# A decoder layer on one core: P times V of four pairs moved ahead of the last product of k, the last norms of three tiles in another form, the first job in another order

## The chip, the cores and the metric

The kernel runs on one core of one Trainium2 chip. The metric is the device time in microseconds (us) of one execution. Engines are named PE (TensorE), DVE (VectorE), ACT (ScalarE), POOL (GpSimd) and SP (SyncE, which here only starts transfers).

## The reference, cut to what matters

```python
h = layer_norm(concat([meta, x]), ln_emb_g, ln_emb_b)      # 16 + 512 tokens of width 1024
qa, ka, va, ga, qi, ki, wi, cq, ckv, kpe, gb = split(h @ w_in)
# branch b: latent attention, 8 heads, dense causal
qb = rms_norm(cq) @ w_uq ; kvb = rms_norm(ckv) @ w_ukv
ob = softmax(qb . kb * scale_b, causal) @ vb
# branch a: 8 heads over the 128 keys that an indexer (qi, ki, wi) picks for each query
la = qa . ka[sel] * scale_a + rel_bias ; oa = softmax(la) @ va[sel]
mixed = concat([oa * silu(ga), ob * silu(gb)])
out = layer_norm(ALPHA * h + mixed @ w_out, ln_post_g, ln_post_b)[:, 16:]
# layer_norm: (y - mean) * rsqrt(var + eps) * g + b, over 1024 columns
```

## The kernel before, in words

All of it is float32. A product of weights and hidden states is made of three products of rounded parts (high times high, high times low, low times high); the parts of the weights lie in `wh` and `wl`, those of the states in `hh` and `hl`. Weight blocks of 128 columns come by SP's queue, ACT makes the high part (line 596), POOL or DVE the low part (line 589). Every engine runs its own instructions in order, and all of them follow one list, `ORDER`, that `schedule()` writes by hand. The entries that matter here:

- `("J", kind, n, m)` is a job: products of PE (line 1503) into a PSUM bank, which ACT and DVE empty. A job of k, `("J", "ka", p, half)`, has 24 products of 264 columns. ACT empties it with four copies (line 935) and DVE with four subtractions (line 1202) into `ks`.
- `("S", g)` are the scores of head g. Heads 0 to 7 are the dense ones (line 1691), heads 8 to 15 the sparse ones (line 1695). DVE adds the mask and takes the minimum (line 1301), `("X", g)` is ACT's exponential, `("R", g)` POOL's division. The scores of an even sparse head wait, on PE, for all of ACT's and DVE's instructions of the last k job of its pair:

```python
                    if g >= HEADS and e == 0:
                        n = max(NJ["ka", p, 1], NJ["qa", p, 0]) + 1
                        pe.wait_ge(job_act, BY_ACT[n])
                        pe.wait_ge(job_dve, BY_DVE[n])
```

- `("TP", g)` and the job `tq` transpose P of head g on PE (lines 1710, 1715, 1717, 1557), and ACT and DVE copy it to `pt`. `("PV", pair, part)` is P times V of two heads, 20 products on PE (line 1740) into `ps_o`, which DVE multiplies with the gate (line 1331).

In the steps g = 7, 9, 11 and 13 the list runs: the products of k for the next pair (and of q, for g = 7), TP and tq of head g - 1, PV of pair 2, 3, 4 or 5, then the scores of the even head g + 1.

The first job (`cq`) is written out ahead of the list. Its states come in eight units of two chunks of 128 columns and two tiles of x. For a unit u PE transposes normed x (`spread`, line 1428), ACT or DVE applies the gain (lines 823, 1075), ACT rounds it (line 833), DVE makes the low part (line 1083). `high(u)` is four products with the high weights (line 1443) and four with the low weights (line 1448), `low(u)` four with the low states (line 1458). Units 4 to 7 need ACT's norm of x tiles 2 and 3 (line 815), and their transposes reuse the banks of units 0 to 3, so `spread(u)` waits for DVE's low part of unit u - 4.

At the end each tile t of 128 tokens takes four jobs `out` (4 to 7), added to `res` by DVE (line 1215), with statistics beside them (lines 1351, 1354, 1357, 1361, 1382). Tiles 0 and 1 then take: DVE reciprocal and minus mean times it (`nmr`, line 1376), ACT scale and shift (line 1034), POOL times gain (line 780), POOL plus bias (line 782). Tile 2 takes: DVE minus mean, times gain, in two halves (line 1369), DVE reciprocal (line 1372), ACT scale (line 1030), POOL plus bias (line 774). Tile 3 stays on DVE (lines 1389, 1392, 1397). SP sends the tiles out.

Of the kernel before, what the change touches and what calls it, by code (L numbers as in the profile page):

```python
# [21 lines left out]
ALU = mybir.AluOpType  # L22
# [9 lines left out]
QT = NQ // P  # L32
# [83 lines left out]
def schedule():  # L116
# [84 lines left out]
    for g in range(2 * HEADS):  # L201
        p = (g % HEADS) // 2
        more = p + 1 < PAIRS

        if g < HEADS:
            jobs = [("va", *va.pop(0)) for _ in range((1, 1, 2, 0, 2, 1, 2, 0)[g])]
            if g % 2 and more:
                jobs = [("qn", p + 1)] + jobs + [("kn", p + 1, 0), ("kn", p + 1, 1)]
                if g == 5:
                    jobs[1:3] = jobs[2:0:-1]  # L210
            if g == HEADS - 1:
                jobs = [("qa", 0), ("ka", 0, 0), ("ka", 0, 1)]
        elif more:
            jobs = [("ka", p + 1, 0), ("ka", p + 1, 1)] if g % 2 else [("qa", p + 1)]
        else:
            jobs = [("out", *outs.pop(0)) for _ in range(6 if g % 2 == 0 else 4)]
        pair = (g - 3) // 2 if g >= 3 and g % 2 else None
        late = pair is not None and g >= HEADS - 1 and more or g == HEADS - 1
        order.append(("S", g))
        if HEADS + 2 <= g < HEADS + 6:  # L220
            order.append(("MIXL", 4 + g - HEADS - 2))
        if g > HEADS and g % 2 and more:
            job(*jobs.pop(0), extra=0)
        if jobs[0][0] == "qn":
            order.append(("QPE", jobs[0][1]))
            job(*jobs.pop(0), extra=0)
        if pair is not None and not late and g < HEADS:
            order += [("PV", pair, 0), ("PV", pair, 1)]
        if g % 2 and g < HEADS - 1:
            while jobs:  # L230
                job(*jobs.pop(0), extra=0)
            pick(2)
        order.append(("X", g))
        if g < HEADS and (g % 2 == 0 or g == HEADS - 1):
            pick(1)
        if pair is not None and not late and g >= HEADS:
            order += [("PV", pair, 0), ("PV", pair, 1)]
        if g >= HEADS and not more:
            for _ in range(3 if g % 2 == 0 else 2):
                job(*jobs.pop(0), extra=int(g % 2 == 0))  # L240
        order.append(("R", g))
        if g == 2 * HEADS - 1:
            need(BLOCKS[0], 1)
        if HEADS <= g < 2 * HEADS - 2:
            order.append(("FOLD", g - HEADS + 2))
        if g < HEADS and g % 2 == 0:
            pick(2)
        if g == HEADS - 1:
            assert not halves
            order += [("MASK",), ("BIAS",), ("FOLD", 0), ("FOLD", 1)]  # L250
        for n, j in enumerate(jobs):
            job(*j, extra=int(j[0] == "out"))
        if g:
            order += [("TP", g - 1), ("J", "tq", g - 1, 0)]
        if late:
            order += [("PV", pair, 0), ("PV", pair, 1)]
        need(BLOCKS[0], 2)
        if HEADS + 1 <= g < HEADS + 5:
            order.append(("MIX", 4 + g - HEADS - 1))
        if g == 2 * HEADS - 2:  # L260
            order += [("MIX", 0), ("MIX", 1)]
# [72 lines left out]
def build(nc, x, meta, ln_emb_g, ln_emb_b, rel_bias, ln_post_g, ln_post_b, weights, gains, onehot, cos_t,  # L334
# [6 lines left out]
    with ctx:  # L341
# [3 lines left out]
        def sem(name):  # L345
            return ctx.enter_context(nc.semaphore(name))
# [118 lines left out]
        h_high = sem("h_high")  # L465
        h_high_act = sem("h_high_act")
        shift = sem("shift")
        ln_pool = sem("ln_pool")
        y_pool = sem("y_pool")
        h_low = sem("h_low")  # L470
        meta_s = sem("meta_s")
# [197 lines left out]
        def _(pool):  # L669
# [39 lines left out]
            for stage, *arg in ORDER:  # L709
# [48 lines left out]
                elif stage == "FOLD":  # L758
                    h = arg[0]
                    pool.wait_ge(bias_in[h], 16)  # L760
                    if h == 0:
                        pool.wait_ge(masked, QT + 1)
                    if h >= 2:
                        pool.wait_ge(s_min, 4 * (HEADS + h - 1))
                    for i in range(QT):
                        s = slice(POFF[i], POFF[i] + NK[i])
                        pool.tensor_tensor(bm[:, h % 2, s], bias[:, h % 4, T - NK[i]:T], mask[:, s],  # L767
                                           ALU.add).then_inc(folded, 1)
                elif stage == "LNC" and arg[0] == QT - 2:
                    t = arg[0]  # L770
                    y = res[:, t, :]
                    pool.wait_ge(post_in, 32)
                    pool.wait_ge(xn_done, t + 1)
                    pool.tensor_tensor(y, y, post_b, ALU.add).then_inc(y_pool, 1)
                elif stage == "LNC" and arg[0] < QT - 1:
                    t = arg[0]
                    y = res[:, t, :]
                    pool.wait_ge(post_in, 32)
                    pool.wait_ge(xn_done, t + 1)
                    pool.tensor_tensor(y, y, post_g, ALU.mult).then_inc(ln_pool, 1)  # L780
                    pool.wait_ge(ln_pool, t + 1)
                    pool.tensor_tensor(y, y, post_b, ALU.add).then_inc(y_pool, 1)


# [1 line left out]
        def _(act):  # L786
# [75 lines left out]
            for stage, *arg in ORDER:  # L862
# [154 lines left out]
                elif stage == "LNB":  # L1017
# [4 lines left out]
                    if t == QT - 1:  # L1022
                        a, b = LAST_PIECES[1]
                        act.wait_ge(y_done, 2)
                        act.dma_start(out[0, NQ - P:NQ, a:b], res[:, t, a:b]).then_inc(y_out, 16)
                    if t == QT - 2:
                        act.wait_ge(centred, 2)
                        act.wait_ge(shift, 7 + 2 * t + 1)
                        y = res[:, t, :]
                        act.activation(y, y, ACT.Identity, scale=rstd[:, t:t + 1]).then_inc(xn_done, 1)  # L1030
                    elif t < QT - 2:
                        act.wait_ge(shift, 7 + 2 * t + 2)
                        y = res[:, t, :]
                        act.activation(y, y, ACT.Identity, bias=nmr[:, t:t + 1], scale=rstd[:, t:t + 1]).then_inc(xn_done, 1)


        @block.vector
        def _(dve):
# [64 lines left out]
            stat(4, 1)  # L1103
            low(0)
            gains_of(3)
            inverse(4, 7)
            low(1)
            low(2)
            low(3)

# [20 lines left out]
            for stage, *arg in ORDER:  # L1131
# [226 lines left out]
                elif stage == "LNB" and arg[0] < QT - 1:  # L1358
# [2 lines left out]
                    dve.bn_stats(st[:, t, 1, :], res[:, t, 512:1024]).then_inc(bn_s, 1)  # L1361
                    dve.wait_ge(bn_s, 10 + 2 * t + 2)
                    dve.bn_aggr(mv[:, t, :], st[:, t, :, :].rearrange("p a b -> p (a b)")).then_inc(stats, 1)
                    if t == QT - 2:
                        dve.wait_ge(post_in, 32)
                        dve.wait_ge(stats, 5 + t + 1)
                        for n in range(2):
                            y = res[:, t, 512 * n:512 * n + 512]
                            dve.scalar_tensor_tensor(out=y, in0=y, scalar=mv[:, t, 0:1], in1=post_g[:, 512 * n:512 * n + 512],
                                                     op0=ALU.subtract, op1=ALU.mult).then_inc(centred, 1)  # L1370
                    dve.wait_ge(root, 8 + t + 1)
                    dve.reciprocal(rstd[:, t:t + 1], rstd[:, t:t + 1]).then_inc(shift, 1)
                    if t == QT - 2:
                        continue
                    dve.wait_ge(shift, 7 + 2 * t + 1)
                    dve.scalar_tensor_tensor(out=nmr[:, t:t + 1], in0=mv[:, t, 0:1], scalar=-1.0,
                                             in1=rstd[:, t:t + 1], op0=ALU.mult, op1=ALU.mult).then_inc(shift, 1)
                elif stage == "LNB":

                    t = QT - 1  # L1380
# [9 lines left out]
                                                 op0=ALU.subtract, op1=ALU.mult).then_inc(ln_s, 1)  # L1390
                    dve.wait_ge(root, 8 + t + 1)
                    dve.reciprocal(rstd[:, t:t + 1], rstd[:, t:t + 1]).then_inc(shift, 1)
                    dve.wait_ge(shift, 7 + 2 * t)
                    dve.wait_ge(ln_s, 2)
                    for a, b in LAST_PIECES:
                        y = res[:, t, a:b]
# [5 lines left out]
        def _(pe):  # L1402
            def busy(count):

                for _ in range(count):
                    pe.transpose(ps_j[:, 1, 0:P], ident[:, :], ident[:, :])
# [21 lines left out]
                        last = pe.transpose(hbank(u)[:, a:a + P], res[:, 2 * (u // 4) + k, c * P:(c + 1) * P], ident[:, :])  # L1428
                last.then_inc(x_t, 1)

            def high(u):

                chunks, s = unit(u)
                a = 256 * (u // 4)
# [6 lines left out]
                for c in chunks:  # L1441
                    for k in range(2):
                        pe.matmul(ps_j[:, k, a:a + 256], wh[:, c, k * P:k * P + P], hh[:, c, s], start=c == 0, stop=False,
                                  skip_group_check=True)
                pe.wait_ge(w_low, u % 4 + 1)
                for c in chunks:
                    for k in range(2):
# [3 lines left out]
            def low(u):  # L1451
# [4 lines left out]
                for k in range(2):  # L1456
# [3 lines left out]
                    if u == DC - 1:  # L1460
                        last.then_inc(job_mm, 1)

            pe.wait_ge(xn_act, 2)
            pe.wait_ge(xn_dve, 1)
            spread(0)
# [4 lines left out]
            high(0)  # L1470
            high(1)
            low(0)
            high(2)
            low(1)
            high(3)
            low(2)
            pe.wait_ge(xn_act, 4)
            spread(4)
            spread(5)
            low(3)  # L1480
            spread(6)
            high(4)
            spread(7)
            low(4)
            high(5)
            low(5)
# [330 lines left out]
```

## Time and profile before

| | |
|---|---|
| median of 3 runs | 332.08 us (332.04 to 332.31) |
| the profiled execution | 332.67 us |
| its span, first to last instruction | 330.8 us |
| mean granted TensorE clock | 0.986 |
| PE busy | 318.6 us (96%) |
| DVE, POOL, ACT busy | 237.4, 201.1, 173.1 us |

The span is what the rows below are read against; the 1.9 us between it and the execution's own time lie around it.

### The profile page before, as it was taken

To read this page: it belongs to the slowest core of one execution; us is meant where nothing else is said; L and a number is where in the kernel's file an instruction comes from. 1 tells how busy PE (TensorE), PEld (TensorE's weight loads), DVE (VectorE), ACT (ScalarE), POOL (GpSimd) and SP (SyncE) were. 2 spreads that over 40 slices of the span, in tenths; PEclk is the share of its full clock that TensorE was granted. 3 is DMA by queue.
4 is the path that set the end of the run, shared out by engine and by line. 5 is a ranking of instruction groups with operands and counts; after the bars stand their busy time and mean duration, and the time that the engine had idled before them with its cause. 6 is when DMAs were issued, how large, how long until landed. Compare 5 with 4: busy or idle time off the path is not lost.

```text
span 330.8 us, 6234 instructions
## 1 busy us (share of the span) xinstructions
PE 318.6 (96%) x2128; PEld 277.7 (84%) x2128; DVE 237.4 (72%) x628; ACT 173.1 (52%) x389; POOL 201.1 (61%) x245
## 2 busy tenths in 40 slices
PE   8999999999999999999999999999999999999990
PEld 7789987788778888987988987897978898998990
DVE  5875820269965799989995995568787866564686
ACT  4865853353443355367454753777587653722220
POOL 6551899989422261429430898789869581660552
PEclk9799999999999999999999999999999999999996
DMA  7664432338423022202400052332323110130033
GB/s 236 227 190 183 133 120 81 118 104 283 162 72 120 28 100 81 79 3 79 130 8 10 25 169 97 99 99 85 100 73 96 64 62 5 64 129 0 2 126 128
DMA packets 11997, 32.86 MB, mean 99 GB/s; under 512 B 2440, under 2 KB 2824, under 8 KB 11968
## 3 DMA queue, kind: packets, MB, share of 16 engines
q1 hardware_dynamic: 9232, 26.89, 24.0%
q10 hardware_dynamic: 2736, 5.59, 5.7%
q8 instruction: 17, 0.28, 0.4%
q14 instruction: 12, 0.10, 0.1%
HBM read 29.83 MB, written 4.81 MB: 105 GB/s over the span
## 4 chain that ended last, share of the span: by engine, by line
PE 87%; DVE 6%; issue 2%; POOL 1%; ACT 1%; DMA 1%; DVEq 0%; ACTq 0%; SPq 0%; POOLq 0%
PE ps_j L1503 52%; PE ps_t L1503 7%; PE ps_o L1740 6%; PE ps_s L1691 5%; PE ps_s L1695 3%; PE ps_s L1664 2%; PE ps_t L1710 2%; PE ps_j L1557 2%; PE ps_t L1715 2%; POOL wl L693 1%; DMA res<-in_x 1%; PE ps_j L1580 1%; PE ps_j L1458 1%; PE ps_j L1448 1%; DVE st L1050 1%
## 5 line engine op out<-in xcount | busy, mean ns | idle before, releaser
L589 POOL TENSOR_TENSOR wl<-raw,wh 128x1024 fp32r<-128x1024 f32 (+2 forms) x33 | 78.0, 2371 | 48.6 <-ACT wh L596 48.5
L1503 PE MATMUL ps_j<-hh,wh 128*128 128x512 f32 (+2 forms) x208 | 73.0, 351 | 0.2 <-DVE qs L1171 0.2
L1503 PE MATMUL ps_j<-hl,wh 128*128 128x512 f32 (+2 forms) x208 | 72.5, 348 | 0.0
L1503 PE MATMUL ps_j<-hh,wl 128*128 128x512 f32 (+2 forms) x208 | 72.1, 347 | 0.0
L749 POOL TENSOR_SCALAR pr<-pr,rden 128x528 f32<-128x528 f32 (+1 forms) x64 | 35.1, 567 | 49.1 <-DVE rden L1312 49.1
L1503 PEld LDWEIGHTS ps_j<-hh,wh 128*128 128x128 f32 (+1 forms) x208 | 38.8, 186 | 6.2 <-issue 0.3
L998 ACT ACTIVATE pr<-pr,mn 128x528 f32<-128x528 f32 (+1 forms) x64 | 36.0, 564 | 14.2 <-DVE mn L1301 14.1
L1503 PEld LDWEIGHTS ps_j<-hh,wl 128*128 128x128 f32 (+1 forms) x208 | 38.8, 187 | 5.1
L1503 PEld LDWEIGHTS ps_j<-hl,wh 128*128 128x128 f32 (+1 forms) x208 | 38.8, 186 | 5.0
L596 ACT ACTIVATE wh<-raw 128x1024 fp32r<-128x1024 f32 (+2 forms) x34 | 34.9, 1041 | 0.8 <-DMA raw<-in_weights 0.8
L767 POOL TENSOR_TENSOR bm<-bias,mask 128x144 f32<-128x144 f32 (+3 forms) x32 | 27.4, 889 | 0.0
L1272 DVE MATCH_REPLACE8 iw<-top,iw 128x512 f32<-128x512 f32 (+2 forms) x42 | 22.6, 542 | 0.0
L1268 DVE MAX8 top<-iw 128x8 f32<-128x512 f32 (+2 forms) x42 | 21.8, 547 | 0.1
L901 ACT ACTIVATE mix<-ps_j 128x512 f32<-128x512 f32 x7 | 4.2, 599 | 30.2 <-PE ps_j L1503 30.2
L1691 PE MATMUL ps_s<-k_b,q_b 96*128 96x240 f32 (+4 forms) x80 | 19.4, 390 | 0.0
L1202 DVE TENSOR_TENSOR ks<-ps_j,ks 64x264 fp32r<-64x264 f32 x32 | 13.8, 431 | 6.6 <-ACT ks L935 5.8
L1503 PE MATMUL ps_j<-wh,mbh 128*128 128x256 f32 x64 | 18.4, 287 | 0.0
L1503 PE MATMUL ps_j<-wl,mbh 128*128 128x256 f32 x64 | 18.1, 283 | 0.0
L1503 PE MATMUL ps_j<-wh,mbl 128*128 128x256 f32 x64 | 18.1, 283 | 0.0
L935 ACT ACTIVATE ks<-ps_j 64x264 fp32r<-64x264 f32 x32 | 12.3, 385 | 9.7 <-PE ps_j L1503 9.0
L1503 PE MATMUL ps_j<-wh,hh 128*128 128x256 f32 x56 | 16.9, 302 | 0.0
L1008 ACT ACTIVATE pt<-ps_t 128x512 f32<-128x512 f32 x16 | 9.4, 590 | 13.6 <-PE ps_t L1710 7.7
(291 smaller groups left out, 849.9 us busy)
## 6 DMA issues: line engine op xcount, KB each, us to landing
raw<-in_weights SPq DMA_DIRECT2D x35, 512.0 KB, 3.4
bias_by_distance<-bias_vector ACTq DMA_DIRECT2D x1, 2624.0 KB, 13.3
bias<-bias_by_distance ACTq DMA_DIRECT2D x8, 264.0 KB, 2.7
res<-in_x SPq DMA_DIRECT2D x4, 512.0 KB, 4.9
out<-res SPq DMA_DIRECT2D x3, 512.0 KB, 2.6
raw<-in_weights SPq DMA_DIRECT2D x5, 256.0 KB, 6.1
pt<-in_ln_emb_g SPq DMA_DIRECT2D x1, 512.0 KB, 5.4
pt<-in_ln_emb_b SPq DMA_DIRECT2D x1, 512.0 KB, 7.0
```

What stands on the lines that cost most here:

```text
L589: eng.tensor_tensor(ring_of(False, b), raw_of(b), ring_of(True, b).bitcast(F32), ALU.subtract).then_inc(done, 1)
L596: act.activation(ring_of(True, b), raw_of(b), ACT.Copy).then_inc(w_high, 1)
L749: pool.tensor_scalar(a, a, rden[:, k, n:n + 1], 1.0, ALU.mult, ALU.mult).then_inc(scaled, 1)
L767: pool.tensor_tensor(bm[:, h % 2, s], bias[:, h % 4, T - NK[i]:T], mask[:, s], ALU.add).then_inc(folded, 1)
L935: act.activation(ks[HD * v:HD * v + HD, e, v, 264 * m:264 * m + 264], bank[HD * e:HD * e + HD, 0:264], ACT.Copy).then_inc(job_act, 1)
L998: act.activation(dst, dst, ACT.Exp, bias=mn[:, k, n:n + 1], scale=-1.0, accum_out=den[:, k, n:n + 1]).then_inc(e_done, 1)
L1202: dve.tensor_tensor(ks[HD - HD * v:P - HD * v, e, v, s], bank[HD * e:HD * e + HD, 0:264], ks[HD * v:HD * v + HD, e, v, s].bitcast(F32), AL ...
L1268: dve.max(top8[:, i, :], a).then_inc(done, 1)
L1272: dve.match_replace(out=a, in_to_replace=top8[:, i, :], in_values=a, imm_value=TAKEN).then_inc(done, 1)
L1503: last = pe.matmul(dst, a, b, start=n == 0 and part[0], stop=n == count - 1 and part[1])
L1691: last = pe.matmul(dst, q_b[:, e, i * P:(i + 1) * P], k_b[:, e, a:b], start=True, stop=True)
L1740: last = pe.matmul(ps_o[HD * e:HD * e + HD, q0:NQ], v[:, j, c:c + HD], pt[:, e, CO[j]:CO[j] + NQ - q0], start=j == 0, stop=j == 4)
```

## The change

Three places are changed. In `schedule()` PV of pairs 2 to 5 goes ahead of the last job of the step, which is the last product of k, and no longer stands behind TP and tq. At the end tiles 0 and 1 take the form that tile 2 had. In the first job `low(1)` goes between the high and the low weights of unit 2 on PE, and ahead of `inverse(4, 7)` (the reciprocal for x tile 3) on DVE; spreads 4 and 5 go ahead of `low(2)`, spread 6 ahead of `low(3)`, and spread 7 ahead of `high(4)`; six transposes whose results are not used (`busy(6)`) go ahead of the first spread.

```diff
         for n, j in enumerate(jobs):
+            if late and n == len(jobs) - 1:
+                order += [("PV", pair, 0), ("PV", pair, 1)]
             job(*j, extra=int(j[0] == "out"))
         if g:
             order += [("TP", g - 1), ("J", "tq", g - 1, 0)]
-        if late:
-            order += [("PV", pair, 0), ("PV", pair, 1)]
         need(BLOCKS[0], 2)
...
                 elif stage == "LNC" and arg[0] < QT - 1:
                     t = arg[0]
                     y = res[:, t, :]
                     pool.wait_ge(post_in, 32)
                     pool.wait_ge(xn_done, t + 1)
-                    pool.tensor_tensor(y, y, post_g, ALU.mult).then_inc(ln_pool, 1)
-                    pool.wait_ge(ln_pool, t + 1)
                     pool.tensor_tensor(y, y, post_b, ALU.add).then_inc(y_pool, 1)
...
-                    if t == QT - 2:
-                        act.wait_ge(centred, 2)
-                        act.wait_ge(shift, 7 + 2 * t + 1)
+                    if t < QT - 1:
+                        act.wait_ge(centred, 2 * t + 2)
+                        act.wait_ge(shift, 7 + t + 1)
                         y = res[:, t, :]
                         act.activation(y, y, ACT.Identity, scale=rstd[:, t:t + 1]).then_inc(xn_done, 1)
-                    elif t < QT - 2:
-                        act.wait_ge(shift, 7 + 2 * t + 2)
-                        y = res[:, t, :]
-                        act.activation(y, y, ACT.Identity, bias=nmr[:, t:t + 1], scale=rstd[:, t:t + 1]).then_inc(xn_done, 1)
...
             gains_of(3)
+            low(1)
             inverse(4, 7)
-            low(1)
             low(2)
...
-                    if t == QT - 2:
-                        dve.wait_ge(post_in, 32)
-                        dve.wait_ge(stats, 5 + t + 1)
-                        for n in range(2):
-                            y = res[:, t, 512 * n:512 * n + 512]
-                            dve.scalar_tensor_tensor(out=y, in0=y, scalar=mv[:, t, 0:1], in1=post_g[:, 512 * n:512 * n + 512],
-                                                     op0=ALU.subtract, op1=ALU.mult).then_inc(centred, 1)
+                    dve.wait_ge(post_in, 32)
+                    dve.wait_ge(stats, 5 + t + 1)
+                    for n in range(2):
+                        y = res[:, t, 512 * n:512 * n + 512]
+                        dve.scalar_tensor_tensor(out=y, in0=y, scalar=mv[:, t, 0:1], in1=post_g[:, 512 * n:512 * n + 512],
+                                                 op0=ALU.subtract, op1=ALU.mult).then_inc(centred, 1)
                     dve.wait_ge(root, 8 + t + 1)
                     dve.reciprocal(rstd[:, t:t + 1], rstd[:, t:t + 1]).then_inc(shift, 1)
-                    if t == QT - 2:
-                        continue
-                    dve.wait_ge(shift, 7 + 2 * t + 1)
-                    dve.scalar_tensor_tensor(out=nmr[:, t:t + 1], in0=mv[:, t, 0:1], scalar=-1.0,
-                                             in1=rstd[:, t:t + 1], op0=ALU.mult, op1=ALU.mult).then_inc(shift, 1)
...
-            def high(u):
+            def high(u, between=None):
...
+                if between is not None:
+                    low(between)
                 pe.wait_ge(w_low, u % 4 + 1)
...
+            busy(6)
             pe.wait_ge(xn_act, 2)
             pe.wait_ge(xn_dve, 1)
             spread(0)
...
             low(0)
-            high(2)
-            low(1)
+            high(2, 1)
             high(3)
-            low(2)
             pe.wait_ge(xn_act, 4)
             spread(4)
             spread(5)
+            low(2)
+            spread(6)
             low(3)
-            spread(6)
+            spread(7)
             high(4)
-            spread(7)
             low(4)
```

## Rows read from the trace of the kernel before

**Rows 1.** The page, busy time and share of the span of each engine.

```profile
PE 318.6 (96%) x2128; PEld 277.7 (84%) x2128; DVE 237.4 (72%) x628; ACT 173.1 (52%) x389; POOL 201.1 (61%) x245
```

**Rows 2.** All waits of PE: for whom, us in total, times, longest.

```profile
PE ps_s L1428 <- DVE res L1067: 0.5, 1, 0.5
PE ps_s L1695 <- issue: 0.5, 2, 0.3
...
PE ps_j L1503 <- DVE qs L1171: 0.2, 1, 0.2
```

**Rows 3.** Chain that ended last, around the scores of heads 8 and 10: start, us, what.

```profile
199.78 3.16 PE ps_j L1503 x24
202.94 0.44 PE ps_t L1710 x4
...
206.60 1.53 PE ps_s L1695 x10
...
222.06 0.44 PE ps_t L1710 x4
...
223.26 2.46 PE ps_o L1740 x20
...
226.00 1.56 PE ps_s L1695 x10
```

**Rows 4.** Timeline, the last k job emptied in steps 7 and 9.

```profile
202.98 1.61 ACT L935 ACTIVATE ks<-ps_j 64x264 fp32r<-64x264 f32 x4 [1.71 <-PE ps_j L1503]
...
203.88 1.82 DVE L1202 TENSOR_TENSOR ks<-ps_j,ks 64x264 fp32r<-64x264 f32 x4 [1.50 <-ACT ks L935]
...
223.19 1.61 ACT L935 ACTIVATE ks<-ps_j 64x264 fp32r<-64x264 f32 x4
...
224.08 1.82 DVE L1202 TENSOR_TENSOR ks<-ps_j,ks 64x264 fp32r<-64x264 f32 x4 [0.72 <-ACT ks L935]
```

**Rows 5.** Timeline, ACT and DVE in the first job.

```profile
17.22 1.25 ACT L815 ACTIVATE res<-res,nmr,rstd 128x1024 f32<-128x1024 f32 x1
...
20.04 0.99 ACT L823 ACTIVATE ps_s<-ps_s,gain 128x256 f32<-128x256 f32 x2 [1.57 <-PE ps_s L1428]
...
21.07 0.60 ACT L833 ACTIVATE hh<-ps_s 128x512 fp32r<-128x512 f32 x1
...
23.48 1.00 DVE L1075 TENSOR_SCALAR ps_s<-ps_s,gain 128x256 f32<-128x256 f32 x2 [1.09 <-PE ps_s L1428]
...
24.39 0.68 DVE L1083 TENSOR_TENSOR hl<-ps_o,hh 128x512 fp32r<-128x512 f32 x1
```

**Rows 6.** Chain that ended last, PE in the first job.

```profile
19.57 0.45 PE ps_s L1428 x4
...
22.53 0.48 PE ps_j L1448 x4
...
28.22 0.48 PE ps_j L1458 x4
```

**Rows 7.** Busy us of each engine in a stretch, granted clock, DMA share, GB/s.

```profile
10.00:16.00 6.00, 5.88 (x38) 5.92 (x39) 5.55 (x13) 5.05 (x11) 4.21 (x5) 0.72 0.55 221
```

**Rows 8.** Timeline of POOL, DVE, ACT and PE at the end.

```profile
317.98 2.40 POOL L782 TENSOR_TENSOR res<-res,pr 128x1024 f32<-128x1024 f32 x1
...
318.53 3.06 DVE L1369 SCALAR_TENSOR_TENSOR res<-res,mv,pr 128x512 f32<-128x512 f32 x2
...
321.76 1.15 ACT L1030 ACTIVATE res<-res,rstd 128x1024 f32<-128x1024 f32 x1 [3.02 <-DVE rstd L1372]
...
322.38 0.28 PE L1503 MATMUL ps_t<-wl,hh 128*128 128x256 f32 x1
...
323.80 0.40 DVE L1215 TENSOR_TENSOR res<-res,ps_t 128x256 f32<-128x256 f32 x1
...
325.07 1.53 DVE L1389 SCALAR_TENSOR_TENSOR res<-res,mv,pr 128x512 f32<-128x512 f32 x2
```

**Rows 9.** Chain that ended last, one half of tile 2.

```profile
314.14 2.86 PE ps_t L1503 x24
```

More of the change, by code:

```diff
@@ L467, in build @@
         shift = sem("shift")
-        ln_pool = sem("ln_pool")
         y_pool = sem("y_pool")
@@ L768, in _ @@
                                            ALU.add).then_inc(folded, 1)
-                elif stage == "LNC" and arg[0] == QT - 2:
-                    t = arg[0]
-                    y = res[:, t, :]
-                    pool.wait_ge(post_in, 32)
-                    pool.wait_ge(xn_done, t + 1)
-                    pool.tensor_tensor(y, y, post_b, ALU.add).then_inc(y_pool, 1)
                 elif stage == "LNC" and arg[0] < QT - 1:
@@ L1025, in _ @@
                         act.dma_start(out[0, NQ - P:NQ, a:b], res[:, t, a:b]).then_inc(y_out, 16)
-                    if t == QT - 2:
-                        act.wait_ge(centred, 2)
-                        act.wait_ge(shift, 7 + 2 * t + 1)
+                    if t < QT - 1:
+                        act.wait_ge(centred, 2 * t + 2)
+                        act.wait_ge(shift, 7 + t + 1)
                         y = res[:, t, :]
                         act.activation(y, y, ACT.Identity, scale=rstd[:, t:t + 1]).then_inc(xn_done, 1)
-                    elif t < QT - 2:
-                        act.wait_ge(shift, 7 + 2 * t + 2)
-                        y = res[:, t, :]
-                        act.activation(y, y, ACT.Identity, bias=nmr[:, t:t + 1], scale=rstd[:, t:t + 1]).then_inc(xn_done, 1)
         @block.vector
@@ L1392, in _ @@
                     dve.reciprocal(rstd[:, t:t + 1], rstd[:, t:t + 1]).then_inc(shift, 1)
-                    dve.wait_ge(shift, 7 + 2 * t)
+                    dve.wait_ge(shift, 7 + QT)
                     dve.wait_ge(ln_s, 2)
```

## The prediction

> **What bounds the kernel now.** I read the page first: PE is busy for 318.6 of 330.8 us [rows 1]. The second view is the list of PE's waits. Between the first job and the end it holds only two entries, 0.5 us ahead of sparse scores (line 1695, two times) and 0.2 us ahead of one product of k [rows 2]. So in the middle PE is never without work: an instruction that makes PE stand still there is paid in full, and work that other engines save there pays nothing. The third view is the chain that ended last. It runs on PE from the first job to the last product, and on DVE behind that. Gains can come from the first job, where PE waits for ACT, DVE and POOL, and from DVE's work behind the last product; losses from any wait put into the middle. The timelines of these three places give the rest.
>
> **PV ahead of the last product of k.** Nothing is added or removed. In each of four steps 20 products of PE, 2.46 us [rows 3], go from behind the last k job, TP and tq to ahead of the k job. DVE's multiplication with the gate moves with them; it waits for PV, which ends before the k product begins, so it holds up nothing queued on DVE. No transfer and no weight block changes its place. At its new place PV waits for nothing new: the copies of P come from the step before, and the product of k that now stands ahead of it gives them 2.9 us more.
>
> What matters is what waits for the k job. The scores of the next even head need all of ACT's and DVE's instructions of it. Step 9: the product ends, and TP begins, at 222.06; TP and tq take 1.20 us, until PV begins at 223.26; PV ends at 225.72; the scores begin at 226.00 [rows 3]. ACT empties the job from 223.19, DVE from 224.08 for 1.82 us, so until 225.90 [rows 4]; the scores follow 0.10 us later. That is the 0.3 us wait of rows 2: already now the scores are held by the emptying of the k job, and not by PE. The emptying takes 2.71 us from ACT's start to DVE's end, and ACT can start 0.04 us behind the product when it is free (202.94 to 202.98 in step 7) [rows 3, 4]. In step 9 ACT started 1.1 us late, since its exponentials come first in its order.
>
> Afterwards the product ends 2.46 us later. ACT's exponentials are then done, so it starts at once: the scores begin 0.04 + 2.71 + 0.10 = 2.85 us behind the product. PE has only TP and tq, 1.20 us, to put there, and stands still for 1.65 us. Counted from the old end of the product the scores begin at 2.46 + 2.85 = 5.31 us instead of 226.00 - 222.06 = 3.94 us: 1.37 us later. Three steps look like this one (9, 11, 13; one is shown): 4.1 us.
>
> In step 7 ACT was free, and the emptying ended at 203.88 + 1.82 = 205.70 [rows 4], hidden by PV, with the scores at 206.60 [rows 3]. Now 5.31 - 3.66 = 1.65 us more, less the wait of 0.16 to 0.2 us for DVE's emptying of q [rows 2], in which PV now runs: 1.5 us. Together **+5.6 us**. Bounds: nothing, if the scores did not wait; and 4 x 1.65 = 6.6 us, if none of the old waits came off. What comes behind gets nothing back, since PE has no later wait that could shrink [rows 2].
>
> **The first job.** PE's blocks of four products take 0.475 us and a spread of four transposes 0.45 us [rows 6]. The norm of x tile 3 ends on ACT at 17.22 + 1.25 = 18.47 [rows 5], and spread 4 cannot begin before. In the old order `low(2)` came first and spread 4 at 19.4 to 19.6; behind it PE waited for ACT's rounding of unit 4 and for DVE. In the new one the transposes go as early as their banks allow, and the low products fill the time. I let PE run without a wait from 18.47 on: 0.05 for the handover, four spreads (1.80), low 2 and 3, and three blocks for each of units 4 to 7, so 14 x 0.475 = 6.65. Is it fed? Unit 4: transposes done 0.6 behind 18.6, then gain 1.0 and rounding 0.6 on ACT [rows 5]: 20.9, and PE comes to it at 21.4. After that two units take PE 2.85 us, ACT 1.0 + 2 x 0.60 = 2.2 and DVE 1.0 + 2 x 0.68 = 2.4 [rows 5]. It is, by some tenths. `busy(6)` costs 6 x 0.11 = 0.65 us, of which PE's wait of 0.52 for DVE [rows 2] hides most; the remaining 0.13 is passed on through ACT, which works without a pause from unit 0 to that norm. If that cover were gone it would be 0.65. The job ends at 18.47 + 0.05 + 0.13 + 1.80 + 6.65 = 27.1 instead of 28.22 + 0.48 = 28.70 [rows 6]: **-1.6 us**. `low(1)` of DVE ahead of the reciprocal costs nothing, for DVE waited there for ACT's root; on PE, `low(1)` fills the wait for POOL's low part. Bounds: 0, if the saving is taken by the next wait, and -2.1, if PE also finds spread 4 ready without any handover and the six transposes are free. The granted clock is 0.72 over 10 to 16 us [rows 7], so 0.28 x 6 = 1.7 us of PE time are lost there; I count nothing for the six transposes keeping it up, because in the new order PE is held until 18.47 by ACT either way.
>
> **The last norms.** Per tile 0 and 1, POOL loses a product of 2.40 us and DVE gains two halves of 0.70 us less a `nmr` of 0.16; ACT loses a tenth. At tile 2 this changes what DVE meets. There its two halves took 3.06 us, from 318.53, while POOL's addition of 2.40 us ran from 317.98 to 320.38; at tile 3 the same two took 1.53, with POOL under only their first 0.3 us [rows 8]. So DVE's instruction stood until POOL's was over; alone I take 1.40 for two. Now POOL has one instruction per tile. From the start of DVE's halves POOL is done after 1.40 + 0.17 (321.59 to ACT's 321.76) + 1.15 + 0.14 + 2.40 = 5.26 us [rows 8], and a tile takes PE 2 x 2.85 = 5.7 us [rows 9]: over 0.4 us before DVE's next halves. At tile 2 DVE is free at 319.9 instead of 321.59 and has no arrears any more when PE's last product ends at 322.38 + 0.28 = 322.66. The last addition then starts at 322.70 instead of 323.80 [rows 8], 1.1 us earlier, and the halves behind it lose 0.13: **-1.2 us**. The new halves for tiles 0 and 1 put DVE 1.4 us behind, which four banks in turn and its pauses of 1 us per job hide; without those PE would wait up to 1.4. Bounds: 0, if POOL's addition meets the halves of tile 2 or 3 again, and -1.7 (3.06 - 1.40).
>
> The Trainium skill (SBUF — State Buffer, section "Who interferes with whom") says that a DVE instruction with two SBUF inputs and a GpSimd instruction that reads SBUF exclude one another, and that the one issued first keeps the shared ports to its end. The trace agrees: the first half at tile 2 came 0.55 us behind POOL's start and ended 0.55 us behind its end. The rule speaks against four more such halves on DVE; by the times above they stand clear of POOL, and were they not, the gain of 1.2 would go to 0.
>
> **The sum.** 5.6 - 1.6 - 1.2 = +2.8 us. Against the profiled execution, 332.67, that is 335.5; the median of the runs is 0.6 lower, so I predict **334.9 us**.
>
> **The rivals.**
> 1. One gain does not arrive: the first job's saving is taken up by a wait behind it (a weight block, or ACT's emptying of the first job), or POOL meets DVE's halves again. For it: the margins are tenths. Against: PE had no wait from 28.7 to 198 us [rows 2], and the blocks come with the job. Time: 334.9 + 1.2 to 1.6 = 336.3. Chance 0.13.
> 2. The clock. PE stands still for 1.65 us, four times, with transposes just before. If the granted clock fell to half for as long as at 10 to 16 us, each fall would cost 1.7 us [rows 7]: 336.6 for one, 341.7 for four. The rows show it granted in full behind waits of up to 0.5 us, and none of 1.65. Chance 0.10, mostly one or two falls.
> 3. Faster. The k job's emptying is not what holds the scores, or PE gets by: then PV moves for nothing, the 0.5 us of waits may go, and the gains stay, 332.1 - 2.8 - 0.5 = 328.8. It decides when the four steps lose under 0.7 us each, so when the emptying behind the product takes under 2.2 us. For it: TP's copies no longer wait for PV, so ACT and DVE have less beside. Against: the code's wait, and 0.10 us between DVE's end and the scores [rows 3, 4]. Chance 0.07.
> 4. The losses and gains nearly cancel (within 0.2%, 0.7 us, which is about what a measurement of this kernel can tell from no change): the steps lose about 1 us each and the gains are at their bounds, 332.1. Chance 0.05.
> The forecast itself has 0.65, and its own range is 333.8 to 335.9.
>
> The range takes rival 1 and one fall of the clock: 333.4 to 336.8. Left out are rivals 3 and 4 and two or more falls, 0.12 + 0.05. Faster 0.07, same 0.05, slower 0.88.
>
> **What the changed profile would show.** PE's waits: four ahead of line 1695 in place of two, 1.5 to 1.7 us each, ending 0.1 us behind DVE's line 1202, and the wait of the k product for DVE's line 1171 gone. The first job ends near 27.1, with no wait of over 0.2 us behind spread 4. At tile 2 line 1369's two halves in 1.4 us instead of 3.06, and the last additions of DVE within 0.1 us of PE's last product. The prediction is wrong if line 1695 waits for under 0.7 us per step, if a clock below 1 shows in the middle, or if PE waits for weights behind the first job.

## The result, and the profile of the changed kernel

The changed kernel takes 335.76 us (median of 4 runs, 335.42 to 336.22) against 332.19 us before (4 runs): slower by 3.6 us, ratio 1.0107, 95% interval 1.0092 to 1.0122. That lies in the range (333.4 to 336.8) and 0.9 us over the predicted 334.9. Its profiled execution has a span of 334.1 us, 3.3 more than before.

Line numbers have moved: the scores of the sparse heads are line 1678 (1695 before), the emptying of k lines 926 on ACT and 1189 on DVE (935, 1202), P times V 1723 (1740), the jobs' products 1486 (1503), tile halves on DVE 1355 and 1370 (1369, 1389), the additions to `res` 1202 (1215).

First the page, then the list of all of PE's waits (us in total, times, longest), which answer to [rows 1] and [rows 2]:

```profile
PE 318.1 (95%) x2134; PEld 276.9 (83%) x2134; DVE 235.2 (70%) x630; ACT 172.8 (52%) x389; POOL 194.6 (58%) x243
```

```profile
PE ps_s L1678 <- ACT pt L920: 6.6, 4, 1.6
PE ps_j L1387 <- POOL ident L671: 1.5, 1, 1.5
PE ps_j L1424 <- ACT hh L824: 0.6, 1, 0.6
PE ps_j L1441 <- DVE hl L1070: 0.2, 1, 0.2
PE ps_j L1486 <- issue: 0.2, 1, 0.2
```

PE is as busy as before to half a us, so most of the added time is in waits: four ahead of line 1678, 6.6 us together, 1.64 each. The wait of 0.2 us for DVE's emptying of q (line 1171 before) is gone. The list puts the four waits down to ACT's line 920, a copy of tq. That is only the release that came last by the profile; the code has PE wait for ACT and DVE on the k job. Here is the chain that ended last around the scores of head 10 (start, us, what), and then the timeline of the same place; they answer to [rows 3] and [rows 4]:

```profile
216.09 2.92 PE ps_j L1486 x24
219.01 2.46 PE ps_o L1723 x20
221.47 3.14 PE ps_j L1486 x24
...
227.44 1.58 PE ps_s L1678 x10
```

```profile
224.63 1.61 ACT L926 ACTIVATE ks<-ps_j 64x264 fp32r<-64x264 f32 x4 [1.60 <-PE ps_j L1486]
...
225.52 1.81 DVE L1189 TENSOR_TENSOR ks<-ps_j,ks 64x264 fp32r<-64x264 f32 x4 [1.58 <-ACT ks L926]
...
227.03 0.28 ACT L920 ACTIVATE pt<-ps_j 128x128 f32<-128x128 f32 x1
...
227.44 1.58 PE L1678 MATMUL ps_s<-ks,qs 128*128 128x240 f32 x10 [1.64 <-ACT pt L920]
```

P times V ends at 221.47, the k product at 224.61. ACT empties it from 224.63, DVE from 225.52 to 227.33, and the scores begin 0.11 us later, 2.83 us behind the product. TP and tq filled 1.20 us of it.

The first job ends at 27.08 us, where the chain goes over to the next job, instead of 28.70 [rows 6]. ACT's norm of x tile 3 stands where it stood; the gain and the rounding of unit 4, for which PE waited before, come 0.8 us earlier than in [rows 5]. First the chain, then ACT's timeline:

```profile
26.61 0.47 PE ps_j L1441 x4
27.08 2.90 PE ps_t L1486 x24
```

```profile
17.23 1.24 ACT L806 ACTIVATE res<-res,nmr,rstd 128x1024 f32<-128x1024 f32 x1
...
19.22 0.99 ACT L814 ACTIVATE ps_s<-ps_s,gain 128x256 f32<-128x256 f32 x2 [0.75 <-PE ps_s L1409]
...
20.24 0.60 ACT L824 ACTIVATE hh<-ps_s 128x512 fp32r<-128x512 f32 x1
```

The granted clock (busy us of the engines in a stretch, then the clock, the DMA share and GB/s) stayed at its upper level of 2.4 GHz in 10 to 16 us, where it was 0.72 of it on average before [rows 7], and also around the long waits in the middle, as in the rows of the third one:

```profile
10.00:16.00 6.00, 5.32 (x44) 4.86 (x42) 5.87 (x14) 5.01 (x11) 4.46 (x5) 1.00 0.48 192
...
245.00:249.00 4.00, 2.35 (x20) 2.14 (x20) 2.33 (x6) 3.26 (x8) 3.94 (x11) 1.00 0.00 0
249.00:253.00 4.00, 4.00 (x22) 3.43 (x21) 3.49 (x14) 2.66 (x9) 3.17 (x2) 1.00 0.12 16
```

The end, timeline of DVE, POOL and PE, for [rows 8]:

```profile
323.06 1.41 DVE L1355 SCALAR_TENSOR_TENSOR res<-res,mv,pr 128x512 f32<-128x512 f32 x2
...
327.24 0.42 DVE L1202 TENSOR_TENSOR res<-res,ps_t 128x256 f32<-128x256 f32 x1 [0.47 <-PE ps_t L1486]
...
328.52 1.41 DVE L1370 SCALAR_TENSOR_TENSOR res<-res,mv,pr 128x512 f32<-128x512 f32 x2
```

```profile
320.26 2.40 POOL L773 TENSOR_TENSOR res<-res,pr 128x1024 f32<-128x1024 f32 x1 [3.27 <-ACT res L1021]
325.94 2.37 POOL L773 TENSOR_TENSOR res<-res,pr 128x1024 f32<-128x1024 f32 x1 [3.28 <-ACT res L1021]
```

```profile
326.92 0.28 PE L1486 MATMUL ps_t<-wl,hh 128*128 128x256 f32 x1
```

POOL's addition for tile 1 ends at 322.66, 0.4 us before DVE begins tile 2's halves, and these take 1.41 us instead of 3.06. PE's last product ends at 326.92 + 0.28 = 327.20, and DVE adds it at 327.24. Before, 1.14 us lay between (322.66, 323.80).

The difference of the two profiles, place by place:

| place | before | after | change of the interval |
|---|---|---|---|
| first job ends | 28.70 | 27.08 | -1.62 |
| scores of head 8 begin | 206.60 | 206.44 | +1.46 |
| scores of head 10 begin | 226.00 | 227.44 | +1.60 |
| scores of head 12 begin | 245.43 | 248.46 | +1.59 |
| scores of head 14 begin | 264.85 | 269.47 | +1.59 |
| last product of PE ends | 322.66 | 327.20 | -0.08 |
| last instruction of DVE ends | 328.26 | 331.59 | -1.21 |

Each row's last column is how much longer the stretch since the row above has become. The sum is +3.33 us, of which the four steps are +6.24.

### The profile page after: what moved, and what is told of

The parts are those of the page before. It is cut to its first block, busy times and chain, and to the rows that moved or that the text cites. A ratio compares the mean times of both kernels' runs of the same rounds, so it can differ in the third digit from the quotient of the medians.

```text
span 334.1 us, 6250 instructions
## 1 busy us (share of the span) xinstructions
PE 318.1 (95%) x2134; PEld 276.9 (83%) x2134; DVE 235.2 (70%) x630; ACT 172.8 (52%) x389; POOL 194.6 (58%) x243
## 4 chain that ended last, share of the span: by engine, by line
PE 90%; DVE 4%; ACT 3%; issue 2%; DMA 1%; DVEq 0%; SPq 0%; ACTq 0%
PE ps_j L1486 55%; PE ps_t L1486 8%; PE ps_o L1723 6%; PE ps_s L1674 5%; PE ps_s L1678 3%; PE ps_s L1647 2%; PE ps_t L1693 2%; PE ps_j L1540 1%; PE ps_t L1698 1%; PE ps_j L1563 1%; PE ps_j L1441 1%; ACT ks L926 1%; DMA res<-in_x 1%; PE ps_j L1431 1%; DVE st L1037 1%
## 5 line engine op out<-in xcount | busy, mean ns | idle before, releaser
L766 POOL TENSOR_TENSOR bm<-bias,mask 128x144 f32<-128x144 f32 (+3 forms) x32 | 25.5, 833 | 0.0
L773 POOL TENSOR_TENSOR res<-res,pr 128x1024 f32<-128x1024 f32 x3 | 7.2, 2391 | 22.0 <-ACT res L1021 22.0
L1678 PE MATMUL ps_s<-ks,qs 128*128 128x240 f32 (+4 forms) x80 | 12.6, 304 | 6.6 <-ACT pt L920 6.6
```

The costliest lines, as they stand in the source:

```text
L1678: last = pe.matmul(dst, qs[:, p % 2, e, i * P:(i + 1) * P], ks[:, e, v, a:b], start=v == 0, stop=v == 1)
```

## The experiments

Each experiment was measured beside the kernel before, on one chip for each group. The first four were one group (before: 332.30 us), the next four another (332.36), the last four a third (332.48). The changed kernel ran beside a kernel before of 332.19, so a difference of 0.1 to 0.3 us between medians of two groups says nothing.

**P times V at its old place, the rest changed (e1).**

```diff
-            if late and n == len(jobs) - 1:
-                order += [("PV", pair, 0), ("PV", pair, 1)]
             job(*j, extra=int(j[0] == "out"))
         if g:
             order += [("TP", g - 1), ("J", "tq", g - 1, 0)]
+        if late:
+            order += [("PV", pair, 0), ("PV", pair, 1)]
```

> The changed kernel with P times V put back behind TP and tq. My theory: all of the loss is in that move, 6.2 us between the first job and the out jobs (four steps of 1.5 to 1.6 us), and the other two parts gain 1.6 and 1.2. So 332.2 - 2.8 = 329.4 us, no wait of PE ahead of the sparse scores of over 0.3 us. Rival: the parts hang together (PE comes 1.6 us earlier to steps that ACT and DVE reach at their own time), so part of the loss stays without the move: over 330.5 us.

Measured: 329.60 us, ratio 0.9915 (0.9901 to 0.9928). The loss is gone and the two gains stay, as expected.

**The move of P times V alone (e2)**, the same lines in the kernel before.

> The kernel before with the move of P times V alone. My theory: 332.2 + 6.2 = 338.4 us, four waits of 1.65 us, and the k product behind P times V takes 3.15 us instead of 2.92. Rival, the parts hang together: the loss differs from 6.2 by over 0.5 us.

Measured: 338.79 us, ratio 1.0194 (1.0180 to 1.0208). All of PE's waits that it has ahead of the sparse scores:

```profile
PE ps_s L1695 <- ACT pt L929: 6.6, 4, 1.6
```

The move costs 6.5 us of medians (6.0 to 6.9 by the interval); with the other changes it costs 6.2 (335.76 against the 329.60 of e1). So the parts do not hang together by more than the noise. In the chain of this profile too the k product behind P times V took 3.14 us in step 9, and the one ahead of it 2.91.

**The first job alone (e3)**, the diff's lines for `high`, `busy(6)`, the order of spreads and DVE's `low(1)`, in the kernel before.

> The kernel before with the first job's new order alone. My theory: the first job ends at 27.1 us instead of 28.7, and all of it reaches the end: 330.6 us. Rival: DVE, which is busy over nine tenths around 120 to 195 us, takes some of it up: 331.2 or more, with a longer wait of PE for DVE's emptying of q in step 7.

Measured: 330.95 us, ratio 0.9957 (0.9944 to 0.9969). A gain of 1.35 us (1.0 to 1.9 by the interval), between my theory's 1.7 and the rival's 1.1. The end of the first job can't be compared between profiles as it stands, because the executions begin differently: DVE's norm of x tile 1 (line 1067 before, 1054 after), for which PE's first spread waits, begins at 8.9 to 10.1 us. Counted from there:

| profile | DVE's norm begins | first spread begins | first job ends | from norm to end |
|---|---|---|---|---|
| before | 9.42 | 10.12 | 28.70 | 19.28 |
| e2, old first job | 9.17 | 9.86 | 28.36 | 19.19 |
| e4, old first job | 8.91 | 9.60 | 28.13 | 19.22 |
| e3, new first job | 9.18 | 10.27 | 27.14 | 17.96 |
| changed kernel | 9.17 | 10.19 | 27.08 | 17.91 |
| e5, new first job | 9.16 | 9.86 | 26.83 | 17.67 |
| e8, without the six transposes | 9.17 | 9.86 | 26.85 | 17.68 |
| e11, old order of spreads | 10.07 | 10.77 | 29.00 | 18.93 |

The new order is worth 1.5 to 1.6 us like for like, and 1.2 to 1.4 in profiles like those of e3 and of the changed kernel, where the first spread came 0.3 us late (see e8). It is not shown that DVE in the middle takes anything of it: PE's wait in step 7 for DVE's emptying of q was 0.2 us here as before, and one new wait of 0.3 us, for ACT's copy of a v job, stood in this profile and in no other.

**The norms alone (e4)**, the diff's lines for `LNB` and `LNC`, in the kernel before.

> The kernel before with the norms of tiles 0 and 1 in the new form alone. My theory: 331.0 us (-1.2), tile 2's halves on DVE 1.4 instead of 3.06 us. Rival: the gain in the changed kernel came from elsewhere (the shifted phase of PE's end to POOL): then within 0.3 us of 332.2.

Measured: 330.76 us, ratio 0.9956 (0.9944 to 0.9968), a gain of 1.5 us (1.1 to 1.9). Timeline of DVE, tile 2's halves and the last addition:

```profile
317.94 1.41 DVE L1355 SCALAR_TENSOR_TENSOR res<-res,mv,pr 128x512 f32<-128x512 f32 x2
...
322.12 0.42 DVE L1202 TENSOR_TENSOR res<-res,ps_t 128x256 f32<-128x256 f32 x1 [0.47 <-PE ps_t L1484]
...
323.40 1.41 DVE L1370 SCALAR_TENSOR_TENSOR res<-res,mv,pr 128x512 f32<-128x512 f32 x2
```

The sum of the three parts alone, 6.5 - 1.35 - 1.5, is 3.65 us; the changed kernel lost 3.6.

**P times V between the last k product and TP (e5).**

```diff
+        if late:
+            order += [("PV", pair, 0), ("PV", pair, 1)]
         if g:
             order += [("TP", g - 1), ("J", "tq", g - 1, 0)]
```

> The changed kernel with P times V between the last product of k and TP, so that it again stands behind the product whose emptying the scores wait for, but ahead of ACT's and DVE's copies of TP. My theory: what counts is how much PE has to do between that product and the scores; it is 3.66 us again, over the 2.83 us that the emptying takes, so 329.5 us, as with the old place, and perhaps 0.1 to 0.3 us per step less, since ACT need not wait for P times V. Rival: P times V must stand behind TP and tq, because the copies of TP compete with the emptying: 331 us or more.

Measured: 329.58 us, ratio 0.9910 (0.9896 to 0.9924), equal to the old place (329.60). So it is not the place of P times V against TP that counts, but that it stands behind the last product of k. In the chain, step 9:

```profile
220.11 2.46 PE ps_o L1723 x20
222.57 0.58 PE ps_t L1693 x4
...
224.03 1.57 PE ps_s L1678 x10
```

tq ends at 223.92, the scores begin at 224.03 and take 1.57 us; in step 7 of the same profile, without a wait, they took 1.34.

**A shorter wait (e6).** The scores of an even head read only the first head's half of `ks`, which the first two instructions of ACT and of DVE write.

```diff
-                    if g >= HEADS and e == 0:
-                        n = max(NJ["ka", p, 1], NJ["qa", p, 0]) + 1
-                        pe.wait_ge(job_act, BY_ACT[n])
-                        pe.wait_ge(job_dve, BY_DVE[n])
+                    if g >= HEADS:
+                        n = NJ["ka", p, 1] + 1
+                        pe.wait_ge(job_act, BY_ACT[n] - 2 * (1 - e))
+                        pe.wait_ge(job_dve, BY_DVE[n] - 2 * (1 - e))
```

> The changed kernel, in which the scores of an even sparse head wait for the first two of ACT's and DVE's four instructions of the last k job (they read only these), and the odd head's wait for all. My theory: the emptying of the part that is needed ends 0.04 + 0.89 + 0.9 + 0.1 = 1.9 us behind the product instead of 2.83, PE's wait falls from 1.65 to about 0.75 us per step, and the time by 4 x 0.9 = 3.6 us to 332.1. Rival: the wait is for something else that ends at the same time (the copies of TP on ACT, which the list of waits names): no change, 335.8.

Measured: 332.43 us, ratio 0.9998 (0.9989 to 1.0006), 3.3 us under the changed kernel and no slower than the kernel before. The waits and, in the timeline of step 9, the emptying and the scores:

```profile
PE ps_s L1678 <- ACT ks L926: 2.9, 4, 0.7
```

```profile
223.50 1.62 ACT L926 ACTIVATE ks<-ps_j 64x264 fp32r<-64x264 f32 x4 [1.62 <-PE ps_j L1486]
...
225.38 1.57 PE L1678 MATMUL ps_s<-ks,qs 128*128 128x240 f32 x10 [0.71 <-ACT ks L926]
...
225.90 0.28 ACT L920 ACTIVATE pt<-ps_j 128x128 f32<-128x128 f32 x1
```

The four waits are 0.7 us each, and the scores begin 1.9 us behind the product (223.48), 0.8 us ahead of the end of ACT's line 920. The emptying of k is the cause; the copy of tq that the list of waits named was not it.

**The shorter wait with P times V at its old place (e7)**, both edits together.

> The same shorter wait with P times V at its old place. My theory: the 0.5 us of waits ahead of the sparse scores go, and nothing else: 329.6 - 0.5 = 329.1 us. Rival: the odd head's wait or another limit takes it up: 329.6.

Measured: 329.55 us, ratio 0.9910 (0.9895 to 0.9924): nothing gained against e1, so the rival holds. The waits ahead of the scores are gone, and another stands in their place in two of the four steps (11 and 13):

```profile
PE ps_j L1540 <- DVE ks L1189: 0.5, 2, 0.2
```

tq writes the bank of the step's first k job, and waits until DVE has emptied it. That job of DVE comes late, behind its minimum and a low part of `mix`; then PE waits there.

**Without the six unused transposes (e8)**, `busy(6)` taken out.

> The changed kernel without the six unused transposes ahead of the first spread. My theory: the granted clock falls to half around 10.7 to 14.1 us as it did before the change, but PE is held until 18.5 us by ACT and POOL either way, so the first job ends within 0.2 us of 27.1: 335.7 us. Rival: the full clock is what ends the first job early: 336.2 us or more, first job ending at 27.6 or later.

Measured: 335.88 us, ratio 1.0096 (1.0083 to 1.0109), the changed kernel's time. The first job ended at 26.85 us. The fall of the clock that I had expected did not come: the granted clock was 1.00 over 10 to 16 us in this profile without them, and so it was in those of e2 and e4, which have the old first job. The fall stands in the profile of before alone, so the effect of the six transposes on it could not be seen. It cost the first job next to nothing there: 19.28 us from DVE's norm to the end, against 19.19 and 19.22.

Nor are the six transposes quite free. In e5 the first spread begins at 9.86 us with them, as without them in e8, and the job ends at the same time. In the profiles of the changed kernel, e1 and e3 it begins at 10.16 to 10.27, and the job ends 0.2 to 0.3 us later. There PE's thirty transposes at the start (line 1387) had taken 6.2 to 6.3 us, against 5.54 in e5, so that the six came later and ran past DVE's norm. The medians show no difference.

**POOL reading under tile 2's halves (e9), and POOL only writing there (e10).** Behind tile 1's addition POOL gets work on a buffer that is no longer used:

```diff
                     pool.tensor_tensor(y, y, post_b, ALU.add).then_inc(y_pool, 1)
+                    if t == QT - 3:     # e9
+                        pool.tensor_tensor(pt[:, 0, 0:D], pt[:, 0, 0:D], pt[:, 0, 0:D], ALU.add).then_inc(folded, 1)
+                    if t == QT - 3:     # e10
+                        for q in range(2):
+                            pool.memset(pt[:, q, 0:PW], 0.0).then_inc(folded, 1)
```

> The changed kernel with one more addition of 128x1024 on POOL (it reads and writes a buffer that nobody uses any more) behind that of tile 1, so that POOL is still reading SBUF when DVE comes to tile 2's halves. My theory: the first half waits for POOL's end as in the kernel before and ends 0.55 us behind it, the two take about 3.2 us instead of 1.41, and 1.1 to 1.4 us of the gain are lost: 337.0 us. Rival: the long halves of the kernel before had another reason: 335.8.

> The same place, but POOL only writes there (two memsets of 128x1344, about 2.7 us). My theory, that only reads of POOL shut DVE's second input out: the halves stay at 1.41 us, 335.8 us. Rival, that any work of POOL does: 337 us, halves of 3 us.

Measured: e9 336.62 us, ratio 1.0120 (1.0102 to 1.0139); e10 335.62, ratio 1.0096 (1.0078 to 1.0113). Timelines of e9, POOL and DVE:

```profile
322.43 1.89 POOL L775 TENSOR_TENSOR pt<-pt 128x1024 f32<-128x1024 f32 x1
```

```profile
322.89 2.65 DVE L1357 SCALAR_TENSOR_TENSOR res<-res,mv,pr 128x512 f32<-128x512 f32 x2
...
327.75 0.40 DVE L1204 TENSOR_TENSOR res<-res,ps_t 128x256 f32<-128x256 f32 x1
```

and of e10:

```profile
322.24 2.37 POOL L776 MEMSET pt<- 128x1344 f32 x2
```

```profile
322.69 1.41 DVE L1358 SCALAR_TENSOR_TENSOR res<-res,mv,pr 128x512 f32<-128x512 f32 x2
...
326.88 0.42 DVE L1205 TENSOR_TENSOR res<-res,ps_t 128x256 f32<-128x256 f32 x1 [0.48 <-PE ps_t L1489]
```

With a POOL instruction that reads, begun 0.46 us ahead, the halves took 2.65 us; with memsets over the same stretch 1.41. The extra addition took 1.89 us, not 2.40, so the loss is smaller than I wrote (0.9 us against the changed kernel and 1.0 against e10, instead of 1.1 to 1.4). The mechanism is the one of the forecast, and e10 shows that it takes a POOL instruction that reads.

**The old order of spreads (e11)**, the rest of the first job as changed.

```diff
+            low(2)
             pe.wait_ge(xn_act, 4)
             spread(4)
             spread(5)
-            low(2)
-            spread(6)
             low(3)
-            spread(7)
+            spread(6)
             high(4)
+            spread(7)
             low(4)
```

> The changed kernel with low(2) ahead of spread 4, spread 6 behind low(3) and spread 7 behind high(4) again; the six transposes and the two moves of low(1) stay. My theory: the gain of the first job is in the order of the spreads; it ends at 28.0 us instead of 26.9 to 27.1, with waits of 0.4 to 0.5 us for ACT's line of unit 4 and DVE's of unit 5, and the time is 336.9. Rival: low(1) ahead of the low weights and of the reciprocal brings it: 335.8 to 336.1.

Measured: 336.89 us, ratio 1.0126 (1.0104 to 1.0148), 1.1 us above the changed kernel and 1.3 above e10 of the same group. Most of the first job's gain is in the order of the spreads. In the chain PE's old waits are back, for ACT's rounding of unit 4 and DVE's low part of unit 5:

```profile
21.39 0.61 ACT hh L824
...
22.13 0.72 PE ps_j L1424 x4
...
24.81 0.60 DVE hl L1070
...
25.45 0.73 PE ps_j L1441 x4
...
28.53 0.47 PE ps_j L1441 x4
```

The job ended at 29.00 us in an execution whose beginning was 0.9 us later (DVE's norm at 10.07 instead of 9.17), so at 28.1 like for like: 18.93 us from the norm, 1.26 more than e5, of the 1.5 to 1.6 of the whole. The remaining 0.3 us would be the two moves of `low(1)`, which no run tried alone.

**P times V between the k product and TP, with the shorter wait (e12)**, the edits of e5 and e6 together.

> P times V between the last product of k and TP, and the shorter wait of the even head's scores. My theory: no wait of PE is left ahead of the sparse scores, 0.1 us off each of three steps against the same order with the full wait (329.58): 329.3 us. Rival: DVE is late with the step's first k job, so the wait goes to tq as it did with P times V at its old place: 329.6.

Measured: 328.68 us, ratio 0.9882 (0.9863 to 0.9900). It is faster than both kernels, by 3.8 us (1.2%) than the one before. In step 9 (chain):

```profile
220.17 2.46 PE ps_o L1723 x20
222.63 0.59 PE ps_t L1693 x4
...
223.98 1.33 PE ps_s L1678 x10
```

No wait is left ahead of the scores, and they take 1.33 us instead of 1.57. Neither edit does anything alone against the old place and the full wait of e1 (e5, e7); together they give 0.9 us. I had expected 0.3, from the visible wait of 0.1 us; by the chains each removed wait of 0.10 to 0.13 us takes 0.24 us of slower start with it, in three steps. In e7 the scores stand directly behind P times V and take 1.53 us without a wait too, so there was no slower start to win.

## Why the prediction was right, and where its sum was off

**The move of P times V: right in mechanism and order, 5.6 us said, 6.24 measured** (6.5 of medians in e2). The four waits were said to be 1.65 us and were 1.64; the scores begin 2.83 us behind the product (2.85 said), 0.11 us behind DVE (0.10 said). The mis-sized term is the k product behind P times V, which I took at the 2.92 us it had behind another k product. It takes 3.14 (221.47 to 224.61), 0.22 more, three times; that is 0.66 us, and the three steps lost 1.60, 1.59 and 1.59 instead of 1.37. In the kernel before this slow start was there once too, in the scores behind P times V (1.53 and 1.56 us in [rows 3], against 1.33 for scores behind tq). Now PE pays it twice per step, behind P times V and again behind the wait. In step 7, where 1.46 us were measured for 1.5, the k product had followed a wait before and had started slowly then too (3.16 us, [rows 3]), so it lost nothing.

**The first job: right in mechanism, its size in part by luck; -1.6 said, -1.62 in the profile, -1.35 in medians (e3).** It ended at 27.08 (27.1 said). e11 shows the order of the spreads as the cause of most of it. But the two profiles do not begin alike: DVE's norm began 0.25 us earlier in the one of the changed kernel, so only 1.37 of the 1.62 us are the new order. The six transposes, priced at 0.13, held the first spread up by 0.33 there (10.19 instead of 9.86). The earlier beginning and this delay nearly cancel, so ACT's norm of x tile 3, from which the forecast counts, ended at 18.47 in both. The clock was rightly counted as nothing.

**The norms: right, -1.2 said, -1.21 in the profile, -1.5 in medians (e4).** e9 and e10 show that POOL's reading is what had stopped DVE. The new halves for tiles 0 and 1 stood clear of POOL (its addition for tile 0 ended at 316.99, tile 1's halves began at 317.38), and PE did not wait.

**The rivals.** Rival 1 fell: both gains arrived, in e1 together (2.7 us). Rival 2 fell: the granted clock showed 1.00 in the 4 us around the wait and in the 4 us behind it, for all four. Rival 3 and rival 4 asked for losses under 0.7 or about 1 us per step; they were 1.5 to 1.6. The sum of 2.8 against the 3.3 of the profiles is the 0.6 us of slow starts, less a tenth; the 3.6 of the medians has 0.2 us more, which is no more than single executions differ by.

## What to carry to other kernels

Independent work of the engine that sets the end belongs behind the product whose emptying the next product waits for, not ahead of it; count what lies between the two against the time from the product's end to the last emptying instruction (here 2.83 us, against 1.20 with P times V moved away and 3.66 with it). Where a wait covers more than the next product reads, shorten it first; an order and a wait that each bring nothing alone can bring something together. The name beside a wait is the release that came last, so read the wait in the code before naming the cause.

## What the runs showed of the hardware that was not expected

PE starts slowly behind a wait, even one of 0.10 us (e5), and behind the products of P times V, whose weights are 64 columns wide instead of 128. The next group of products takes 0.20 to 0.26 us more: the k product 3.14 to 3.16 instead of 2.90 to 2.93, the scores 1.53 to 1.58 instead of 1.33. The four transposes of TP behind P times V take 0.59 instead of 0.44. This time counts as busy, and no list of waits has it. Whether it is the width of the weights that does it behind P times V was not tried.

PE's granted clock stayed full through four waits of 1.64 us. Over 10 to 16 us it was 0.72 in the profile of before, but 1.00 in those of the kernels with the same first job (e2, e4) and of the changed kernel without the six transposes (e8); what made it fall in that one execution is open.
